# A streaming encoder step on Trainium2: three PSUM bank pairs for the turned tiles, and copies, splits and bank waits in another order

## The reference

```python
x = x + mix @ w_out[layer]                                       # "output product"
h = _rmsnorm(x, norm_ffn[layer])
x = x + jnp.square(jax.nn.relu(h @ w_ff1[layer])) @ w_ff2[layer]  # "feed-forward", hidden 4096
```

## Time and profile before

| | |
|---|---|
| median of 3 runs | 2989.7 us (2987.18 to 2994.84) |
| the profiled execution | 2983.44 us |
| its span, first to last instruction | 2981.6 us |
| busy: PE | 2779.4 us (93%) |
| busy: PE weight load | 2531.8 us (85%) |
| busy: DVE | 1507.9 us (51%) |
| busy: POOL | 1273.6 us (43%) |
| busy: ACT | 1018.1 us (34%) |
| mean granted TensorE clock | 0.972 of full speed |

### The profile page before, as it was taken

How to read it: one execution, slowest core, us unless ns; L and a number is a source line. 1 busy time by engine, 2 the same in 40 slices (tenths; PEclk the granted TensorE clock), 3 DMA queues, 4 the chain that set the end, 5 groups by cost and what they waited for, 6 DMA issues and landing times.

```text
span 2981.6 us, 43355 instructions
## 1 busy us (share of the span) xinstructions
PE 2779.4 (93%) x17102; PEld 2531.8 (85%) x17102; DVE 1507.9 (51%) x2110; ACT 1018.1 (34%) x1631; POOL 1273.6 (43%) x743
## 2 busy tenths in 40 slices
PE   7999988898869999999999999899978999999998
PEld 7999977687768888988888989887867898889987
DVE  5500236575336665566644310088345566765565
ACT  5412336453333232232324311255232232233232
POOL 2112354233245555656532131186225555555642
PEclk9999999999989999999999999999989999999999
DMA  4112230133363455443543131113445533455442
GB/s 147 42 33 75 87 114 2 65 121 133 98 213 145 161 204 204 169 162 124 209 148 115 39 128 56 62 49 102 146 131 222 208 151 137 169 208 200 178 168 83
DMA packets 189533, 388.40 MB, mean 130 GB/s; under 512 B 26629, under 2 KB 144737, under 8 KB 178916
## 3 DMA queue, kind: packets, MB, share of 16 engines
q1 hardware_dynamic: 179344, 347.21, 32.4%
q0 software_dynamic: 9936, 39.37, 3.5%
q10 hardware_dynamic: 132, 0.13, 0.0%
HBM read 329.84 MB, written 56.79 MB: 130 GB/s over the span
## 4 chain that ended last, share of the span: by engine, by line
PE 66%; issue 10%; DVE 9%; POOL 6%; DMA 4%; ACT 3%; PEld 1%; SPq 0%; DVEq 0%; POOLq 0%; PEldq 0%; ACTq 0%
PE ps L546 16%; PE ps L892 16%; PE ps L969 13%; PE ps L594 7%; PE ps L1051 3%; PE ps L556 3%; DMA units_r<-operands 2%; POOL split L1238 2%; DVE units L1364 2%; DVE units L1333 2%; PE ps L2279 1%; DVE units_r L1348 1%; PE ps L2260 1%; DVE small L3183 1%; POOL split L668 1%
## 5 line engine op out<-in xcount | busy, mean ns | idle before, releaser
L1238 POOL TENSOR_TENSOR split<-raw,split 128x1024 fp32r<-128x1024 f32 x218 | 554.3, 2555 | 561.7 <-ACT split L1092 541.1
L892 PE MATMUL ps<-units_r,split 128*128 128x288 f32 x5376 | 727.5, 297 | 33.7 <-ACT units L1102 26.0
L892 PEld LDWEIGHTS ps<-units_r,split 128*128 128x128 f32 x5376 | 721.9, 189 | 39.2 <-ACT units L1102 26.5
L546 PE MATMUL ps<-units_r,split 128*128 128x384 f32 x2736 | 481.2, 336 | 2.9 <-DVEq L296 2.6
L546 PEld LDWEIGHTS ps<-units_r,split 128*128 128x128 f32 x2736 | 478.1, 189 | 4.0 <-issue 2.9
L1092 ACT ACTIVATE split<-raw 128x1024 fp32r<-128x1024 f32 x218 | 228.5, 1055 | 408.3 <-PE ps L892 127.9
L1353 DVE TENSOR_TENSOR units<-units,ps 128x512 f32<-128x512 f32 x434 | 284.2, 683 | 114.1 <-PE ps L969 112.7
L969 PE MATMUL ps<-split,units_r 128*128 128x512 f32 x1344 | 309.2, 389 | 0.0
L969 PEld LDWEIGHTS ps<-split,units_r 128*128 128x128 f32 x1344 | 252.3, 188 | 52.4
L276 POOL TENSOR_TENSOR split<-raw,split 128x2048 fp32r<-128x2048 f32 x30 | 138.7, 4626 | 328.9 <-ACT split L271 328.9
L969 PE MATMUL ps<-split,spare_r 128*128 128x512 f32 x1008 | 235.6, 389 | 0.0
(11 more groups left out here) (457 smaller groups left out, 3747.8 us busy)
## 6 DMA issues: line engine op xcount, KB each, us to landing
units_r<-operands SPq DMA_DIRECT2D x76, 2304.0 KB, 8.8
raw<-w_ff SPq DMA_DIRECT2D x128, 512.0 KB, 3.8
raw<-w_in_even SPq DMA_DIRECT2D x14, 1024.0 KB, 5.1
operands<-split SPq DMA_DIRECT2D x24, 512.0 KB, 4.8
raw<-w_in_odd SPq DMA_DIRECT2D x12, 1024.0 KB, 5.2
raw<-w_out SPq DMA_DIRECT2D x8, 1024.0 KB, 8.6
operands<-units_r SPq DMA_DIRECT2D x16, 512.0 KB, 3.7
units<-x_prompt SPq DMA_DIRECT2D x3, 1536.0 KB, 11.6
```

The lines of the kernel that those rows point to most:

```text
L546: last = pe.matmul(ps[:, bank + n, 0:GN], weights(slab, a, k, c0, P), h[b][:, k, n * GN:(n + 1) * GN], start=(k == 0 and q == 0), stop=(k ...
L892: last = pe.matmul(ps[:, bank + f, 0:HN], right_slot(base, slot, a)[:, COLS * k + P * f:COLS * k + P * (f + 1)], x[:, b, k, HN * g:HN * (g ...
L1238: pool.tensor_tensor(right_slot(base, slot, 1), src, right_slot(base, slot, 0), ALU.subtract).then_inc(lo_ready, 1)
```

## The change

Turned tiles get three bank pairs, 2-3, 4-5 and 6-7 (`turned_bank`), instead of two; the nine last output products share banks 0 and 1 and wait for the add two jobs back. DVE's `turned_tile(p - 1)` follows `scale(p)`, where `turned_tile(p - 2)` stood ahead of it; ACT's sums follow at once behind `high`. The sums of the last two groups get places of their own (`stage_place`), so that only groups 1 and 2 wait for the stores of the one before. The copy of row half 2 and the split of weight slot 2 (`third`) move ahead: in block 0 into `out_act`, in the others to the end of the block before, and there the copy comes before the split of slot 3. `MIXED2` of block 0 is loaded as soon as its own parts are stored. Inside a block PE waits for ACT's copy of row half 14 before the ninth's first product, where it waited for DVE's square of it, and DVE makes the difference `s3` ahead of the sums of row halves 11 and 12.

```diff
+        def out_bank(j):
+            return j % 4 if j < OUT_TAIL else j % 2
...
                     high(p - 1)
-                if p >= 2 and (p - 2) in SECOND:
-                    sums(SECOND[p - 2])
+                    if p - 1 in SECOND:
+                        sums(SECOND[p - 1])
             copy(0)
             high(NT - 1)
             sums(len(GROUPS) - 1)
+            copy(0, g=1, half=2)
+            for g in (2, 3):
+                act.wait_ge(*stored_groups(layer, g))
+            third(0, 0)
...
             for g in range(len(GROUPS)):
...
-                for c, high in enumerate((2, 3, 4, 4)):
+                for c, high in ((1, 2), (2, 4), (0, 4), (3, 4)):
                     pool.wait_ge(sums_hi, done + high)
-                    c = (1, 0, 2, 3)[c]
                     pool.tensor_tensor(sum_rows(layer, g, c, 1), sum_values(layer, g, c), sum_rows(layer, g, c, 0), ALU.subtract).then_inc(sums_lo, 1)
...
                 if j >= 4:
-                    pe.wait_ge(w_add, len(OUT_JOBS) * layer + j - 3)
-                pair_product(pe, ps[:, j % 4, 0:width], lambda a, k, n: mixed_tile(layer, a, k, n), j, base, right).then_inc(w_y, 1)
+                    pe.wait_ge(w_add, len(OUT_JOBS) * layer + j - (3 if j < OUT_TAIL else 1))
+                pair_product(pe, ps[:, out_bank(j), 0:width], lambda a, k, n: mixed_tile(layer, a, k, n), j, base, right).then_inc(w_y, 1)
...
                 pe.wait_ge(xs_ready, NT * k + p + 1)
-                if p >= 2:
-                    group = [g for g, both_ in enumerate(GROUPS) if p - 2 in both_][0]
+                if p >= 3:
+                    group = [g for g, both_ in enumerate(GROUPS) if p - 3 in both_][0]
                     pe.wait_ge(sums_made, MADE0 + 4 * (len(GROUPS) * layer + group + 1))
...
-                    last = pe.transpose(turn_banks(p)[:, c], xs[:, p % 2, c * P:(c + 1) * P], ident)
+                    last = pe.transpose(turned_bank(p)[:, c], xs[:, p % 2, c * P:(c + 1) * P], ident)
...
-                if g:
+                if g in (1, 2):
                     dve.wait_ge(*stored_groups(layer, g - 1))
...
             for p in range(NT):
                 add(OUT_TAIL + p)
-                if p >= 2:
-                    turned_tile(p - 2)
...
                 scale(p)
-            turned_tile(NT - 2)
+                if p >= 1:
+                    turned_tile(p - 1)
             turned_tile(NT - 1)
...
+        def turned_bank(p):
+            b = 2 + 2 * (p % 3)
+            return ps[:, b:b + 2, :].rearrange("p b (c t) -> p (b c) t", c=4)
...
         def stage_place(layer, g, c, of):
             e = 3 * g + (0, None, 1, 2)[c]
-            a, s = STAGE_AT[e % 4]
-            w = 64 if GROUPS[g][0] == GROUPS[g][1] else P
+            if g == len(GROUPS) - 1:
+                at = (6, 2)[layer] * UNIT + 4 * T + 1024 * (e % 3)
+                return span(at, at + 1024, of)
+            few_rows = GROUPS[g][0] == GROUPS[g][1]
+            if few_rows and c == 3:
+                return FKST if of is pairs else FKST_r
+            a, s = STAGE_AT[1 if few_rows else e % 4]
             at = 2 * SLAB * (((MLP0, MLP1)[layer] + 1) % 2) + SLAB * a + 1024 * s
-            rows = lend[:, at:at + 8 * w] if of is pairs else split.rearrange("p n a c -> p (n a c)")[:, at:at + 8 * w]
-            return rows
+            at, n = (at + 512 * (c == 2), 512) if few_rows else (at, 1024)
+            return lend[:, at:at + n] if of is pairs else split.rearrange("p n a c -> p (n a c)")[:, at:at + n]
...
-        ROW_BANKS, SUM_BANKS = (2, 0), (4, 6)
+        ROW_BANKS, SUM_BANKS = (0, 2), (4, 6)
...
-        SUMS_FIRST, SUMS_LAST = (0, 1, 2, 3), (2, 3, 0, 1)
+        SUMS_FIRST = (0, 1, 2, 3)
...
-            def hidden_rows(blk):
+            def hidden_rows(blk, late):
...
                 pe.wait_ge(turned_rows, ROWS0 + groups * (layer + 1))
+                pe.wait_ge(sums_made, MADE0 + 4 * (groups * layer + groups - 1))
                 row_half(pe, base, 0, b21, 1, ROW_BANKS[1])
...
                 for g in range(2):
-                    summed(9 + g)
+                    summed(9 + late + g)
                     row_half(pe, base, 2, b21, g, SUM_BANKS[g], True)
...
                 left(2)
-                pe.wait_ge(ff_sq, blk * SQUARES + (squares + 15))
+                pe.wait_ge(ff_relu, blk * COPIES + (copies + 8))
                 product(7, ninth(0), 0, True, False, False)
...
                 product(6, ninth(0), 1, True, True, True).then_inc(ff_y, 1)
...
                 for j, n in enumerate(LAST_TILES):
                     if j == 4:
-                        pe.wait_ge(ff_sq, squares + LASTB * SQUARES + 14)
+                        pe.wait_ge(ff_relu, copies + LASTB * COPIES + 8)
...
+            def third(blk, after):
+                weight_in(act, layer, 1, 1, blk, 1 + 2 * after)
+                weight(blk, 2, right_raw(base, 1, 1), 1, after)
+            return first, copy, third, weight
...
                 def added(count):
...
-                for r in range(2):
-                    act.wait_ge(stage_out[r][0], stored_groups(layer, len(GROUPS) - r - 1)[1])
-                weight_in(act, layer, 1, 1, blk, 1)
-                weight(blk, 2, right_raw(base, 1, 1), 1)
                 added(1)
                 weight(blk, 3, right_raw(base, 0, 0), 1)
-                copy(blk, g=1, half=2)
                 added(2)
                 weight(blk, 0, right_raw(base, 0, 1), 2)
...
                 weight(blk, 1, right_raw(base, 1, 0), 7)
-                squared(13)
+                squared(9)
                 left_high(a2[:, 0], left_third(layer))
...
                 first(blk, 1)
                 act.wait_ge(ff_lo, blk * LEFTS + (lows + LEFTS))
+                third(blk, 1)
                 copy(blk, 1)
+                copy(blk, 1, g=1, half=2)
...
                 hidden_part(blk, 0, 1, 9, 5, 5, ROW_BANKS)
                 low(2, half_of(left_ninth[:, 1, 0:2]), samples_of(plain, 0), half_of(left_ninth[:, 0, 0:2]))
-                hidden_part(blk, 1, 1, 11, 3, 9, SUM_BANKS)
                 squared(8)
                 dve.tensor_tensor(s3, p11, p21, ALU.subtract).then_inc(ff_sq, 1)
+                hidden_part(blk, 1, 1, 11, 3, 10, SUM_BANKS)
                 hidden_end(blk, 0)
                 low(3, a2[:, 1], s3, a2[:, 0])
                 hidden_end(blk, 1)
...
                 for g in range(len(GROUPS)):
                     sp.wait_ge(turned_rows, ROWS0 + done + g + 1)
                     straight(MIXED, 1, 0, g)
-                    for count, c in enumerate((1, 0, 2, 3)):
+                    for count, c in enumerate((1, 2, 0, 3)):
+                        if g == len(GROUPS) - 1 and c == 0:
+                            sp.wait_ge(straight_out, STRAIGHT0 + 32 * len(GROUPS) * (layer + 1))
+                            sp.wait_ge(*stored_groups(layer, g - 1))
+                            sp.wait_ge(stored_groups(layer, g)[0], stored_groups(layer, g)[1] - 32)
+                            multiplied(0, 2)
+                            operand_load(MIXED2)
                         sp.wait_ge(sums_lo, SUMS_LO0 + 4 * (done + g) + count + 1)
                         if c == 1:
...
                             stored(which, src, g).then_inc(stored_groups(layer, g)[0], 16)
-                for g in (-2, -1):
-                    sp.wait_ge(*stored_groups(layer, len(GROUPS) + g))
-                sp.wait_ge(straight_out, STRAIGHT0 + 32 * len(GROUPS) * (layer + 1))
...
                 def inside(blk):
                     made(blk, 5)
                     quarter_load(layer, base, 1, 1, second_weights(layer, blk, 1, 1))
-                    multiplied(blk, 2)
-                    operand_load(MIXED2)
+                    if blk:
+                        multiplied(blk, 2)
+                        operand_load(MIXED2)
+                    else:
+                        sp.wait_ge(*stored_groups(layer, len(GROUPS) - 1))
                     made(blk, 6)```

What the engines' lists hold at the three places that the prediction speaks of, as the built programs have them. First DVE in the last nine output products, around the adds of tiles 3 and 4. Before:

```order
L716 TENSOR_TENSOR units<-units,ps 128x512 [waits w_y]
L749 TENSOR_TENSOR lend<-ps,units 128x512 [waits norm_hi]
L750 TENSOR_TENSOR units<-units,ps 128x4x128
L752 TENSOR_TENSOR lend<-lend,ps 128x512 [waits par_tr]
L753 TENSOR_TENSOR units_r<-ps,units_r 128x4x128
L756 TENSOR_TENSOR lend<-ps,lend 128x512 [waits par_tr]
L721 RECIPROCAL small<-small 128x1 [waits sq_done]
L726 SCALAR_TENSOR_TENSOR spare<-units,small,sel 128x1024 [waits tr_ready,root_ready]
L716 TENSOR_TENSOR units<-units,ps 128x512 [waits w_y]
```

19 lines of the change are left out of this document (9 added, 10 removed).

## The result

| | before | after |
|---|---|---|
| median | 2988.9 us (4 runs, 2987.18 to 2994.84) | 2895.7 us (4 runs, 2893.97 to 2900.87) |
| profiled execution, its span | 2983.44, 2981.6 us | 2894.4, 2892.6 us |
| mean granted TensorE clock | 0.972 | 0.985 |

The ratio is 0.9688, with a 95% interval of 0.9669 to 0.9706. I had forecast 2899 us, 2885 to 2932. The two profiles differ by 89.0 us of span, the medians by 93.2.

The account below looks back on a forecast made before the run. PE was taken as the bound. Terms -34.1, -35.4, -28.6 and +7.1 sum to -91.0 us; from the profiled 2983.44 that gives 2892.4, plus 6.3 for the median: 2899 us, range 2885 to 2932.

Parts of the forecast that it names:

- Part 1: Tails of both layers: earlier sums and a third bank pair end the turns' stalls and slow clock; -34.1 us.
- Rival (a): Tail: stores landing 3 us later stall two of three turns in each layer; 2921 us, chance 0.20.
- Part 2: Opening of block 0, both layers: a 3.4 us stall for POOL's split stays, most waiting goes; -35.4 us.
- just hidden: Block 0: the load of `MIXED2` ends at 24.4 us from the opening, row half 7 would begin at 25.7.
- rival (b): Inside blocks: POOL begins before `s3`, row half 11's add ends 2.3 us late, x 14; 2931 us, chance 0.08.
- Part 3: The ninth in fourteen blocks: all 25.4 us of stalls and 3.2 us of slow clock go; -28.6 us.
- the ninth's bank: The ninth: with `s3` earlier, ACT copies row half 14 as it ends and PE waits for nothing; -28.6 us.
- Rival (c): Inside blocks: `s3` waits out POOL's four operations, row half 13 starts 10.5 us late; 3046 us, chance 0.04.
- Part 4: Fourteen blocks: slot 3's later split delays `MIXED2`, which lands 0.7 us late in each; +7.1 us.

Follow-up runs that it names:

- two_pairs: Changed kernel with two bank pairs for turned tiles again, a turn waiting for the sums of the tile two before; 2903.3 us.
- late_order: Changed kernel, three bank pairs kept, but DVE's rows and sums and ACT's copies of the sums one turn later, as before; 2914.9 us.
- load_behind: Changed kernel with block 0's load of `MIXED2` behind all stores again, as before; 2900.8 us, ratio 0.9661 to 0.9703.
- only_s3: Kernel before with only `s3` made ahead of the adds and squares of row halves 11 and 12; 2951.0 us.
- only_bank_wait: Kernel before with only the ninth's wait changed, to ACT's copy of row half 14 instead of DVE's square; 2974.1 us.
- old_bank_wait: Changed kernel with the ninth waiting for DVE's square of row half 14 again, `s3` still early; 2902.6 us, ratio 0.9673 to 0.9713.

## Why the prediction was right, step by step

**Part 1, the turns: -37.5, forecast -34.1.** The mechanism held. The 1.5 us a layer that I took off for late stores didn't come: DVE stood for a store once in layer 0, 0.46 us, and twice in layer 1, 1.12 and 0.25 us, and PE not at all. PE is now the bound of this stretch, at 6.36 us for a product and a turn against my 6.4. Rival (a) is out. two_pairs and late_order show that the third pair and the new order do the same work: either alone gives 16 to 17 of the 19 us in each layer.

**Part 2, the opening: -31.2 from turn 7 to the first ninth, forecast -37.9** (-35.4 and the 2.5 us of the two first ninths). The window to row half 7 came out at 24.65 us, 1.05 below my 25.7: the stall for POOL's split was 2.70 instead of 3.4, and the clock behind it didn't fall in layer 0 (granted 1.00), where I had 2.2 us for it, while `MIXED2`, "just hidden", was late by 1.16. What I missed lies around this window. The opening itself waits for the last add, 1.07 and 1.48 us, because the sums of tile 6 now stand ahead of it on DVE. And row half 13 waits 2.59 and 2.53 us for the add of row half 11, with 1.3 us of slower clock once. There ACT had stood 7.12 us for a quarter of the weights, and POOL and `s3` came at the same time:

```profile
853.50 2.40 POOL L1256 TENSOR_TENSOR split<-raw,split 128x1024 fp32r<-128x1024 f32 x1 [11.12 <-ACT split L1109]
855.98 2.43 POOL L1285 TENSOR_TENSOR raw<-raw 128x1024 f32<-128x1024 f32 x1
...
856.11 3.39 DVE L1381 TENSOR_TENSOR units<-units 128x1024 f32<-128x1024 f32 x1
859.42 1.41 DVE L1347 TENSOR_TENSOR units<-units,ps 128x576 f32<-128x576 f32 x2
```

POOL's instruction begins 0.13 us ahead of `s3`, which ends 1.09 us behind it. This is rival (b), in two blocks of fourteen; I had looked only at a steady block. late_order and load_behind price the order of the sums and the early load; no run undoes the early split of slot 2 or the separate places of the sums alone, so how the rest of the 31.2 us divides between them is argued from the timeline and not shown.

**Part 3, the ninth: right in size, wrong in its cause.** Before to only_s3, twelve blocks give -28.9 us; for these twelve I had 22.9 of stalls and 3.2 of clock, 26.1. (5.83 x 0.71 is 4.1 and not 4.2; a ninth at full speed takes 4.24 to 4.4 us.) That the size came out so near is in part luck: against the second profile of before the same blocks give -32.3, since six ninths ran slow there, and in the median only_s3 is 38.6 us ahead. But the step "the ninth's bank", with the wait on the copy as what frees PE and `s3` as a means to it, has the weights wrong: the wait alone gives 5.9 of 28.9 (only_bank_wait; 19.3 against 38.6 in the medians), and with `s3` early it gives nothing (old_bank_wait). The place of `s3` gives all of it without the wait. My margins for that place were exact:

```profile
947.96 1.22 DVE L1381 TENSOR_TENSOR units<-units 128x1024 f32<-128x1024 f32 x1
949.10 0.75 DVE L1347 TENSOR_TENSOR units<-units,ps 128x576 f32<-128x576 f32 x1
...
948.62 2.82 POOL L1256 TENSOR_TENSOR split<-raw,split 128x1024 fp32r<-128x1024 f32 x1 [2.77 <-ACT split L1109]
```

`s3` is ahead of POOL by 0.66 us (forecast 0.65) and takes 1.22 instead of 3.41; POOL's split takes 2.82 instead of 2.38. In both places the one that starts first runs through and the other pays: in block 0 `s3` took 3.39 us behind POOL's start, here POOL pays 0.44. The Trainium skill, page "SBUF — State Buffer", section "SBUF: two separate sides", states the same rule, and these rows agree with it. Rival (c) is out.

**Part 4, slot 3's split: +10.7 in twelve blocks, forecast +6.1 for these** (7.1 for fourteen). It is the difference of the changed kernel's six-block windows to those of only_s3. The delay of the issue was 0.69, as forecast (0.64). The term that was mis-sized is the wait in each block: the fourteen waits at row half 7 came to 14.4 us, 1.03 each where I had 0.7. I had taken the median landing, though in my own block PE stood 0.63 us for the load already, so that 0.63 + 0.64 would have been the price there; and 1049.85 + 8.8 - 1058.05 is 0.6 and not 0.7. A smaller part is that with the ninths' stalls gone nothing gives the loads time any more (only_s3, with the old order of the splits, waits 3.5 us at these fourteen places, 2.75 before), and one of the stalls, 2.19 us in layer 1, brought 1.5 us of slower clock.

The errors, -3.4, +6.7, -2.8 and +4.6, make +5.1 us; the -3.35 of the start, which isn't the change's, takes back most of that. The forecast's sum, -91.0, stands against -89.0 of the profiles and -93.2 of the medians. The last term was off as well: I put the median 6.3 us above the profiled execution, as it was before, and it came out 1.3 above. So the total is nearer than its parts, and that is luck.

## What to carry over

When PE waits for one result of an engine, look at everything that engine delivers next before putting a price on that wait: here the earlier release alone moved most of it (5.9 of 28.9 us came off), and moving the long instruction out of the way, into a gap where the engine idles anyway, removed it. A step moved by half a microsecond costs little while something later in the loop stalls and hides it; when the same change removes that stall, price the step as if the loop had no slack. Check margins in the first pass of a loop as well as in a steady one: its loads and neighbours come at other times. And before trusting one profile as the baseline, take a second: here the clock behind equal stalls made the same kernel some 6 us longer.
